# Prompt attention with its eight query tiles in the order 4, 0, 5, 1, 6, 2, 7, 3

## What is computed

```python
def body(args):                       # one of 8 query blocks of 128
    qi, gi, s0 = args
    ...
    return _nsa_core(qi, qpos, gi, kc, vc, cend, ks_blk, vs_blk, kwi[:, :, 0], kwi[:, :, 1], wpos)
o = lax.map(body, (qb, gb, starts))
...
o = (gates[..., 0:1] * oc + gates[..., 1:2] * osel + gates[..., 2:3] * ow)
...
s = jnp.einsum('bqhd,bmhd->bhqm', mq, mkv[:, :, 0]) * (HEAD_DIM ** -0.5)
p = jax.nn.softmax(s, axis=-1)
o = jnp.einsum('bhqm,bmhd->bqhd', p, mkv[:, :, 1])
```

## Time and profile before

| | |
|---|---|
| median of 3 runs | 2625.35 us (2620.64 to 2625.82) |
| profiled execution, its own time | 2625.98 us |
| span of the profiled execution | 2624.2 us |
| mean granted TensorE clock | 0.983 |
| PE busy | 2534.1 us (97%) |
| DVE, ACT, POOL busy | 913.6, 640.1, 492.0 us |
| the prompt's attention, first scores to last values | 571.9 to 877.8 us of the span |

### The profile page before, as it was taken

One profiled execution on the slowest core, in us unless ns is written; L12 is line 12 of the kernel. 1 busy time (PEld: TensorE's weight loads), 2 busy tenths in 40 slices (PEclk: granted clock), 3 DMA queues, 4 the chain that ended last, 5 costly groups with the idle time before them and its releaser, 6 DMA issues.

```text
span 2624.2 us, 44708 instructions
## 1 busy us (share of the span) xinstructions
PE 2534.1 (97%) x18212; PEld 2106.2 (80%) x18212; DVE 913.6 (35%) x2523; ACT 640.1 (24%) x1639; POOL 492.0 (19%) x485
## 2 busy tenths in 40 slices
PE   9999988989999889999999999999999999999997
PEld 4555565446666644599999999999999999999996
DVE  2223143227766433425223222223323232323222
ACT  1212132226766423311111111111111111111110
POOL 0000032010000202412222311322313131313121
PEclk9999988989999989999999999999999999999998
DMA  5000076022000453597777887888989999999896
GB/s 209 13 24 22 15 176 125 0 94 98 1 1 1 145 146 113 181 333 243 270 237 259 276 296 275 267 311 278 307 314 301 331 312 332 310 324 317 310 326 246
DMA packets 282076, 534.07 MB, mean 204 GB/s; under 512 B 52463, under 2 KB 94295, under 8 KB 281660
## 3 DMA queue, kind: packets, MB, share of 16 engines
q1 hardware_dynamic: 231244, 470.69, 50.6%
q0 software_dynamic: 33648, 47.92, 8.3%
q10 hardware_dynamic: 16976, 12.56, 1.8%
HBM read 492.75 MB, written 43.48 MB: 204 GB/s over the span
## 4 chain that ended last, share of the span: by engine, by line
PE 61%; DMA 1%; DVE 0%; POOL 0%; issue 0%; SPq 0%; ACT 0%; POOLq 0%; ACTq 0%; DVEq 0%
PE eo L2348 37%; PE eo L2374 19%; PE eo L2199 4%; DMA cache_rows<-summed_rows 0%; DMA out_xp<-w_up 0%; DMA slot_tokens_gates<-token_gate_s,dest_s 0%; PE etp L2223 0%; POOL summed_rows L2136 0%; PE erp L2245 0%; DMA summed_rows<-window_rows,row_index_cur 0%; SPq L2109 0%; POOL x_rows L2130 0%; DMA x_rows<-h_rows,row_index_cur 0%; ACT hT_e L2402 0%; PE erp L2237 0%
## 5 line engine op out<-in xcount | busy, mean ns | idle before, releaser
L2348 PE MATMUL eo<-rg_oret,cache_rows 128*128 128x128 f32 (+19 forms) x4096 | 505.3, 286 | 0.5 <-DVE rg_oret L2654 0.5
L2348 PE MATMUL eo<-rg_oret,w_up 128*128 128x128 f32 (+19 forms) x4096 | 505.2, 286 | 0.0
L2348 PEld LDWEIGHTS eo<-rg_oret,cache_rows 128*128 128x128 f32 x4096 | 502.1, 191 | 1.3 <-DVE rg_oret L2654 1.3
L2348 PEld LDWEIGHTS eo<-rg_oret,w_up 128*128 128x128 f32 x4096 | 502.1, 191 | 0.0
L2374 PE MATMUL eo<-rg_oret,mixT 128*128 128x128 f32 (+19 forms) x3968 | 493.2, 286 | 0.0
L2374 PEld LDWEIGHTS eo<-rg_oret,mixT 128*128 128x128 f32 x3968 | 489.2, 191 | 1.1
L2673 DVE TENSOR_SCALAR window_rows<-eo,b_up_cur 128x128 f32<-128x128 f32 (+19 forms) x256 | 93.7, 366 | 993.3 <-PE eo L2348 993.3
L2136 POOL DMA_INDIRECT summed_rows<-window_rows,row_index_cur x149 | 235.3, 1579 | 1053.6 <-ACT window_rows L2454 1017.6
L364 PE MATMUL zp<-w_in,xnT 128*128 128x512 f32 (+3 forms) x816 | 303.3, 528 | 1.6 <-DVE xnT L598 1.0
L2465 ACT ACTIVATE window_rows<-window_rows 128x128 f32<-128x128 f32 (+19 forms) x256 | 82.4, 322 | 850.6 <-DVE window_rows L2673 850.6
L364 PEld LDWEIGHTS zp<-w_in,xnT 128*128 128x128 f32 x816 | 148.9, 193 | 134.3 <-issue 115.0
(11 more groups left out here) (493 smaller groups left out, 2113.3 us busy)
## 6 DMA issues: line engine op xcount, KB each, us to landing
cache_rows<-in_w_up SPq DMA_DIRECT2D x64, 2048.0 KB, 15.3
w_up<-in_w_up SPq DMA_DIRECT2D x64, 2048.0 KB, 12.5
mixT<-in_w_down SPq DMA_DIRECT2D x64, 2048.0 KB, 12.3
w_in<-in_w_in SPq DMA_DIRECT2D x3, 2048.0 KB, 12.1
x<-in_x_prompt SPq DMA_DIRECT2D x8, 512.0 KB, 3.9
w_up<-in_x_prompt SPq DMA_DIRECT2D x8, 512.0 KB, 3.5
summed_rows<-window_rows SPq DMA_DIRECT2D x8, 512.0 KB, 2.7
h_rows<-h SPq DMA_DIRECT2D x8, 512.0 KB, 3.6
```

The lines of the kernel that those rows point to most:

```text
L2348: mm = nc.tensor.matmul(up[c % 2][:, h, :N], U[c // 4][:, h, kk, w0:w0 + P], hT[:, kk, :N], start=(kk == 0), stop=(kk == KC - 1))
```

## The change

The loop over the tiles runs over a list. Everything that counted tiles by their number (the output buffer in use, the tile whose buffer must be free, the probabilities' buffer two jobs back) now counts by the place in the list. No instruction's work changes, and the sizes and numbers of matmuls, copies and exponentials are the same; their order is not.

```diff
     UNITS = []
-    for qt in range(PT):
+    TILES = [4, 0, 5, 1, 6, 2, 7, 3]
+    place = {qt: n for n, qt in enumerate(TILES)}
+    ahead_of = lambda qt: TILES[place[qt] - 1]
+    for qt in TILES:
         UNITS.append(("C", qt, 0))
...
-    last_q = [last_step[("W", qt, HPG - 1)] for qt in range(PT)]
+    last_q = {qt: last_step[("W", qt, HPG - 1)] for qt in TILES}
...
-                ob = op[(qt + (kind == "M")) % 2]
+                ob = op[(place[qt] + (kind == "M")) % 2]
...
-                    if g == 0 and qt:
-                        pe.wait_ge(s_o, 2 * qt - 1)
+                    if g == 0 and place[qt]:
+                        pe.wait_ge(s_o, 2 * place[qt] - 1)
...
-                        act.wait_ge(s_t, last_step[("M", qt - 1, 0)] + 1)
+                        act.wait_ge(s_t, last_step[("M", ahead_of(qt), 0)] + 1)
...
-                job = HPG * qt + c - 2
+                job = HPG * place[qt] + c - 2
...
-            ends = [e for qt in range(PT) for e in (last_step[("M", qt, 0)], last_q[qt])]
+            ends = [e for qt in TILES for e in (last_step[("M", qt, 0)], last_q[qt])]
```

More of the change, by code:

```diff
@@ L1204, in values @@
                 src = PTs[y % NPT]
-                ob = op[(qt + (kind == "M")) % 2]
+                ob = op[(place[qt] + (kind == "M")) % 2]
                 if kind == "C":
                     g = part[0]
-                    if g == 0 and qt == 0:
+                    if g == 0 and place[qt] == 0:
                         pe.wait_ge(s_re, NT)
-                    if g == 0 and qt:
-                        pe.wait_ge(s_o, 2 * qt - 1)
+                    if g == 0 and place[qt]:
+                        pe.wait_ge(s_o, 2 * place[qt] - 1)
                     mm = nc.tensor.matmul(ob[64 * g:64 * g + 64, :], k.vc[:, DB, 64 * g:64 * g + 64], src[:NCMP, :], start=True, stop=False)
                 elif kind == "M":
-                    if part[0] == 0 and qt:
-                        pe.wait_ge(s_o, 2 * qt)
+                    if part[0] == 0 and place[qt]:
+                        pe.wait_ge(s_o, 2 * place[qt])
                     for h in range(4):
@@ L1260, in exponentials @@
                 if kind == "M":
-                    if qt:
-                        act.wait_ge(s_t, last_step[("M", qt - 1, 0)] + 1)
+                    if place[qt]:
+                        act.wait_ge(s_t, last_step[("M", ahead_of(qt), 0)] + 1)
                     for h in range(4):
@@ L1268, in exponentials @@
                     return
-                job = HPG * qt + c - 2
+                job = HPG * place[qt] + c - 2
                 if job >= 0:
-                    act.wait_ge(s_t, last_step[(kind, job // HPG, job % HPG)] + 1)
+                    act.wait_ge(s_t, last_step[(kind, TILES[job // HPG], job % HPG)] + 1)
                 w, b = width(kind, qt), base(kind)
@@ L1324, in maxima @@
                     link(red(cst[:, 0, :], s3))
-                    if qt:
-                        dve.wait_ge(s_t, last_step[("C", qt - 1, 0)] + 1)
+                    if place[qt]:
+                        dve.wait_ge(s_t, last_step[("C", ahead_of(qt), 0)] + 1)
                     ins = nc.vector.tensor_tensor(Pc[:], s3, bc(cst[:, 0, :], NCMP), ALU.add)
@@ L1363, in output @@
             def output(n):
-                qt = n // 2
+                qt = TILES[n // 2]
                 q = slice(qt * P, qt * P + P)
@@ L1367, in output @@
                     dve.wait_ge(s_pv, last_step[("M", qt, 0)] + 1)
-                    nc.vector.tensor_copy(k.mixT[:, 6:8, q], op[(qt + 1) % 2][:, 0:256].rearrange("p (i x) -> p i x", i=2)).then_inc(s_o, 1)
+                    nc.vector.tensor_copy(k.mixT[:, 6:8, q], op[(place[qt] + 1) % 2][:, 0:256].rearrange("p (i x) -> p i x", i=2)).then_inc(s_o, 1)
                 else:
                     dve.wait_ge(s_pv, last_q[qt] + 1)
-                    nc.vector.tensor_copy(k.mixT[:, 0:4, q], op[qt % 2][:].rearrange("p (c x) -> p c x", c=HPG)).then_inc(s_o, 1)
-            ends = [e for qt in range(PT) for e in (last_step[("M", qt, 0)], last_q[qt])]
+                    nc.vector.tensor_copy(k.mixT[:, 0:4, q], op[place[qt] % 2][:].rearrange("p (c x) -> p c x", c=HPG)).then_inc(s_o, 1)
+            ends = [e for qt in TILES for e in (last_step[("M", qt, 0)], last_q[qt])]
             nc.vector.tensor_copy(identb[:], C[:, at["ident"]])
```

## The result

| | median | runs | ratio to before |
|---|---|---|---|
| before | 2624.41 us | 6 (2620.12 to 2628.85) | |
| tile order 4, 0, 5, 1, 6, 2, 7, 3 | 2636.06 us | 6 (2631.59 to 2643.38) | 1.0052 (1.0038 to 1.0067) |

The kernel became slower by 11.7 us (0.5%). The forecast was 2632.8 us, 7.4 us slower, with a range of 2624 to 2641.

A forecast was written before the change was run, and what follows sets the result against it. PE's own work was taken to bound narrow tiles, waits for exponentials to idle it in wide ones. Terms of +4.4 - 1.7 + 0.2 + 5.1 + 5.7 + 0 - 8.0, plus 1.7 for a dip, gave +7.4: 2632.8 us, range 2624 to 2641.

The forecast's parts named there:

- tile 4 first: Wide tile now starting the prompt's attention, partly at the low clock: +4.4 us, bounds +1 and +8.
- tile 0: Narrow tile: -6.4 us of start-up, +2.7 for five key tiles, +2.0 of wait, so -1.7 us.
- tile 1: Narrow tile: less two waits and a clock dip, plus three key tiles and a 1.7 us wait, so +0.2 us.
- tile 2: Narrow tile: less 0.9 us of idle, plus 8 key tiles (4.3) and a 1.7 us wait, so +5.1 us.
- tiles 5, 6, 7: Wide tiles: fewer key tiles taken over but fewer passed on, so 0 us, bounds 0 and -2.2.
- tile 3 and drain: Last narrow tile +5.7 us with 8 key tiles more; work after the last tile -8.0 us, down to 4.9.
- one dip: PE's clock at half for 3.4 us behind one of four new waits: +1.7 us, bounds 0 and 6.8.
- wait for C: In tiles 0 to 3, PE idles before C's transposes, its scaling queued behind L's maxima on DVE: 1.7 to 2.0 us.
- rival (a): Clock falls behind most new waits and returns late in tile 4; three dips more, 2637.9 us; chance 0.17.
- (b): Wide tiles are bound by PE's work and shrink with what they don't take over: about 2627.0 us; chance 0.16.
- (c): Pending parts are hidden after all in narrow tiles; faster, 2618.1 us with all of them hidden; chance 0.06.
- (d): Low clock for a shorter time at the start, tile 4 +1 in place of +4.4: 2629.4 us; chance 0.13.

The follow-up runs named there:

- a_scale_first: The new tile order with one DVE edit, scaling of C ahead of L's maxima in the unit behind a C unit: 2626.87 us, ratio to before 1.0005.
- a_two_held: The new tile order with two pending parts held back from the C unit to stand between the scores of L and W: 2629.10 us, ratio to before 1.0011.
- a_again: The changed kernel run once more without any edit: 2637.45 us, ratio to before 1.0050.

## Why the prediction held, term by term

| term | predicted | measured in the profile after |
|---|---|---|
| tile 4 first | +4.4 | 46.9 us, +2.7 (over six executions +1.1 to +5.1) |
| tile 0 | -1.7 | 23.6, +0.8, with a dip |
| tile 1 | +0.2 | 26.6, +2.1, with a dip |
| tile 2 | +5.1 | 34.6, +7.3, with a dip |
| tiles 5, 6, 7 | 0 | -0.2, -0.3, +1.1 |
| tile 3 and drain | +5.7 - 8.0 | 44.1 in place of 44.4, -0.3 |
| one dip | +1.7 | in the tiles above |
| phase | +7.4 | +13.1 |

**The mechanism and its place were right.** The batches of pending parts are not hidden in narrow tiles, where PE has no idle time to give. The wait for C was forecast at 2.0, 1.7, 1.7 and 1.8 us and came at 1.89, 1.68, 1.73 and 1.78, ended by DVE's scaling of `rT`. `a_scale_first` (1.0005) and `a_two_held` (1.0011) show that this wait and the clock behind it are most of a loss of 1.0052, and `a_scale_first` can't be told from the kernel before.

**The clock was the term that was too small.** One dip was counted, and three came in the profiled execution, two in `a_again`. That is rival (a) in part: it was given four dips and a loss of 12.5 us, and the measured 11.7 us is nearer to it than to the forecast of 7.4. Its late clock in tile 4 did not come in the profiled execution. The argument that held it down was that waits of 1.55 us behind M units leave the clock alone. The waits for C differ little in length. `a_two_held` shows a dip behind waits of 0.42 and 0.65 us, so the length of a single wait does not decide; what does was not settled. The Trainium skill's rule (TensorE: Matmul & The Clock Gate, "HAM oscillation — how this bites in real kernels"), that only idle gaps well longer than these cost the clock, does not agree with these traces, and the measurement decides: dips that cost some 1.7 us each came behind waits of 1.68 to 1.89 us, and went when the waits were filled.

**Smaller terms were off, and some errors cancelled.** The end was forecast too cheap by 2.0 us. In the turns behind tile 3's last unit PE waits 0.52 us for a scaling and 0.28 us for an eviction, where the drain of tile 7 had one wait of 0.42 us; another 0.45 us is lost inside the batch of 14 key tiles, for an eviction that stands behind C's exponentials on ACT:

```profile
848.04 0.63 PE L1200 MATMUL PTp<-tables_sb,P 128*128 128x128 f32 x4 [0.45 <-ACT rg_oret L1293]
...
882.58 0.66 PE L1200 MATMUL PTp<-tables_sb,P 128*128 128x128 f32 x4 [0.52 <-DVE P L1363]
883.52 0.63 PE L1200 MATMUL PTp<-tables_sb,P 128*128 128x128 f32 x4 [0.28 <-ACT rg_oret L1293]
```

The rest of the 2.0 us was not followed up, nor were the 0.8 and 0.5 us by which tiles 0 and 2 exceed the forecast with its wait and a dip added.

Tile 7 was said to stay as it is and took 1.1 us more. It takes over fewer parts, so C's values fall into the first W unit, ahead of M's scores, which start 5.4 us behind W's scores in place of 4.5. The bounds for tiles 5 to 7 together were 0 and -2.2 and they came at +0.6, so the sign was wrong as well. Against these two, tile 4's start cost 1.7 us less than forecast in this execution: M's scores began 16.1 us behind the first scores in place of 18.3. The clock had risen at 576.7 us, ahead of W's scores at 579.12, and was low again only from 580.1 to 583.5. The forecast also has a slip there: 4.1 us of work with half of it at the low clock takes 6.2 us, not the 5.0 that lie between its W and M scores, so by its own terms tile 4 was +5.6. The term of +4.4 is inside what the six executions show, and its bounds of +1 and +8 hold them all.

**The other rivals.** (b), wide tiles that shrink with the work taken from them, did not come: tiles 5 and 6 are shorter by 0.2 and 0.3 us, while PE is busy 1.9 and 1.1 us less in them. (c), hidden batches, did not come. (d), a short start-up, is seen in two executions of six (+1.1 us), both of edited kernels, and does not turn the result.

## What to carry over

An operation that stands first in an engine's program order sets the pace even when its input comes last: before reordering work, look at what stood between a producer and its consumer by accident, and move the operation whose input is ready ahead of the one that waits. Work that is queued for a later moment is only hidden in stretches where its own engine idles; for the drain here it was PE itself that was busy. And a short stall of TensorE can be charged twice, as here in 7 of 12 cases, once as idle time and once at the lower clock behind it.

## What the runs showed of the hardware beyond that

Waits of 1.7 to 1.9 us on TensorE were followed by some 3.4 us at half the clock in some executions and not in others of the same program: 3 of 4 in one, 2 of 4 in the other. Filling the same waits with repeated matmuls kept the clock at 1.00 through all four narrow tiles, and by the medians, whose intervals overlap, the kernel was faster although it did more work, 2631.88 against 2637.45 us. The changed program's executions spread over 12.5 us in six runs of `a_again` (2631.8 to 2644.3), wider than the 9.2 us in 24 runs of the kernel before on the same chip (2620.6 to 2629.8), and the length of tile 4 and the number of dips differ between its traces too. That the one is the cause of the other was not tested.
